# Head norms and rotations of windowed attention laid between the chunks of a Mamba-2 convolution, in a two-layer hybrid backbone on one core

## The reference, cut to what matters

```python
def mixer_cd(h_lat, h_ctx, row, col, ...):
    q_l, k_l, v_l, z_l, xbc_l, dt_l = jnp.split(h_lat @ w_in, cuts, axis=-1)
    q_c, k_c, v_c, z_c, xbc_c, dt_c = jnp.split(h_ctx @ w_in, cuts, axis=-1)
    k_c = rmsnorm(heads(k_c, 2), k_head_g)
    q_lh = rope_2d(rmsnorm(heads(q_l, 8), q_head_g), row, col)
    k_lh = rope_2d(rmsnorm(heads(k_l, 2), k_head_g), row, col)
    attn_l = window_attention(q_lh, k_lh, heads(v_l, 2), k_c, v_c, sink)
    # the other half: u = silu(conv4(xbc)); x (512), B (256), C (256) = split(u)
    # two directions, chunks of 128: y = (C B^T * decay) (x dt) + D x
    y = rmsnorm((ys[0] + ys[1]) * silu(z), norm_g)
    return concat(attn_l, y) @ w_out
```

## Time and profile before

| | |
|---|---|
| median of 3 runs | 1686.78 us (1683.6 to 1687.5) |
| the profiled execution's own time | 1687.27 us |
| its span, first to last instruction | 1685.5 us |
| mean granted TensorE clock | 0.865 of full speed |
| busy: TensorE, VectorE, ScalarE | 74%, 32%, 24% |
| scan's stage, heads' stage, attention (from their first instructions) | 152.6, 22.5, 60.3 us |

### The profile page before, as it was taken

One profiled execution on the slowest core, in us unless ns is written; L12 is line 12 of the kernel. 1 busy time (PEld: TensorE's weight loads), 2 busy tenths in 40 slices (PEclk: granted clock), 3 DMA queues, 4 the chain that ended last, 5 costly groups with the idle time before them and its releaser, 6 DMA issues. The chain is left out here.

```text
span 1685.5 us, 34940 instructions
## 1 busy us (share of the span) xinstructions
PE 1249.5 (74%) x14230; PEld 727.4 (43%) x14231; DVE 541.3 (32%) x1492; ACT 405.3 (24%) x932; POOL 39.3 (2%) x83
## 2 busy tenths in 40 slices
PE   3897888795799997686762999488497675556552
PEld 2454665543465554343431565244255342223221
DVE  0537555515322221121115444863521110111102
ACT  0343224303132321121104123342222221111110
POOL 0001001010000000000002000000000000000000
PEclk8899899997899998899875999758699897777776
DMA  6411988396699999999987210442689999999995
GB/s 254 156 76 45 329 331 305 106 408 254 254 415 428 429 430 428 429 429 429 429 354 256 68 50 0 168 182 88 257 365 428 429 429 429 429 429 429 429 429 217
DMA packets 84160, 515.12 MB, mean 306 GB/s; under 512 B 13917, under 2 KB 18242, under 8 KB 58746
## 3 DMA queue, kind: packets, MB, share of 16 engines
q1 hardware_dynamic: 75248, 489.63, 70.9%
q10 hardware_dynamic: 5146, 13.78, 2.1%
q0 software_dynamic: 3696, 10.73, 1.7%
HBM read 497.10 MB, written 17.01 MB: 305 GB/s over the span
## 5 line engine op out<-in xcount | busy, mean ns | idle before, releaser
L1481 PE MATMUL bank<-sb_ring,sb_scratch 128*32 128x256 f32 x3904 | 271.8, 440 | 150.7 <-DMA sb_ring<-in_moe_w_up 139.3
L1481 PEld LDWEIGHTS bank<-sb_ring,sb_scratch 128*32 128x32 f32 x3904 | 146.4, 126 | 273.6 <-issue 214.2
L1562 DVE TENSOR_TENSOR sb_scratch<-sb_scratch,bank 128x128 f32<-128x128 f32 x88 | 25.4, 288 | 701.2 <-ACT sb_scratch L1515 701.2
L1519 ACT ACTIVATE sb_scratch<-bank 32x256 f32<-32x256 f32 x352 | 131.8, 374 | 273.9 <-PE bank L1491 270.8
L1481 PE MATMUL bank<-sb_scratch 128*32 128x256 f32 x1728 | 117.5, 432 | 63.4 <-DMA sb_scratch<-in_moe_w_up 58.4
L1461 PE MATMUL bank<-sb_h,sb_scratch 128*32 128x256 f32 x2256 | 141.2, 385 | 6.1 <-DVE sb_scratch L1549 6.1
L1515 ACT ACTIVATE sb_scratch<-bank 128x128 f32<-128x128 f32 x88 | 24.4, 277 | 424.5 <-PE bank L1481 424.4
L1491 PE MATMUL bank<-sb_ring,sb_scratch 128*32 128x256 f32 x1856 | 111.5, 380 | 8.6 <-issue 8.2
L1481 PEld LDWEIGHTS bank<-sb_scratch 128*32 128x32 f32 x1728 | 61.5, 124 | 117.9 <-issue 92.7
L1461 PEld LDWEIGHTS bank<-sb_h,sb_scratch 128*32 128x32 f32 x2256 | 75.0, 111 | 54.6 <-DVE sb_scratch L1549 6.6
L1491 PEld LDWEIGHTS bank<-sb_ring,sb_scratch 128*32 128x32 f32 x1856 | 62.7, 110 | 51.2 <-issue 19.0
(11 more groups left out here) (366 smaller groups left out, 1450.4 us busy)
## 6 DMA issues: line engine op xcount, KB each, us to landing
sb_ring<-in_moe_w_gate SPq DMA_DIRECT2D x44, 2048.0 KB, 27.4
sb_ring<-in_moe_w_up SPq DMA_DIRECT2D x44, 2048.0 KB, 32.1
sb_ring<-in_moe_w_down SPq DMA_DIRECT2D x41, 2048.0 KB, 34.5
sb_ring<-in_ada_w SPq DMA_DIRECT2D x20, 2048.0 KB, 14.4
sb_scratch<-in_moe_w_up SPq DMA_DIRECT2D x20, 2048.0 KB, 35.7
sb_scratch<-in_moe_w_gate SPq DMA_DIRECT2D x20, 2048.0 KB, 29.9
sb_scratch<-in_moe_w_down SPq DMA_DIRECT2D x20, 2048.0 KB, 36.2
sorted_out<-sb_scratch ACTq DMA_DIRECT2D x88, 128.0 KB, 6.1
```

The costliest lines, as they stand in the source:

```text
L1481: last = nc.tensor.matmul(c.bank(1, 2, FQ)[MB * q:MB * q + MB, :, :], m.xt[:, k, :], m.gu[j][:, :, k, q * FQ:(q + 1) * FQ], start=k == 0, ...
L1519: last = nc.scalar.activation(m.yb[j][:, q * DQ:(q + 1) * DQ], c.ps[3][MB * q:MB * q + MB, 0:DQ], ACT.Copy)
L1562: v.tensor_tensor(m.hm, m.sg, c.ps[1][:, FQ:2 * FQ], ALU.mult).then_inc(hm_ready, 1)
```

## The change

`swa_heads_stage` is taken out, and its work is put into `project_ssd_stage`; `loads` goes to the attention stage's SyncE. The chunks are in another order: the queries' second, then x, then B and C, then z. TensorE's order becomes: four row units, two query units, x, `cumulate` behind the fourth, B, C, with `turn_inputs` between, then six batches of four head transposes around the four gate units, the products, and a loop without projections. All batches use bank 5, so each waits for ScalarE's copy of the one before. C is projected, copied, convolved and passed through Silu for the 256 latent positions alone. VectorE squares the keys ahead of the convolution, and behind chunks 0, 2, 3, 4 and 5 does one part each of norms and rotations, now for all tiles of a kind together; `work`, their scratch, moves to `ring[0]`. ScalarE takes one Sqrt for all heads behind its second Silu.

```diff
-def conv_channels(c, dst, src, m, w_cols, b_col, width):
+def conv_channels(c, dst, src, m, w_cols, b_col, width, streams=2):
-    out = dst[:, m, :].rearrange("p (s t) -> p s t", s=2)
+    out, src = dst[:, m, :].rearrange("p (s t) -> p s t", s=2)[:, 0:streams], src[:, m, 0:streams]
...
-CHUNKS_CD = [((512, 256), (2304, 16)), ((1280, 512),), ((1792, 512),), ((768, 512),), ((0, 512),)]
+CHUNKS_CD = [((512, 256), (2304, 16)), ((0, 512),), ((1280, 512),), ((1792, 512),), ((768, 512),)]
...
-        self.work = cut(c.ht_flat, 1024, 2, SI)
+        self.work = c.ring[0][:, 6144:6144 + LT * SI]
...
-    ROWS, XBC, GATE, QUERY = 0, 4, 12, 16
+    QUERY, XBC, GATE = 4, 6, 14
+    def wide(j):
+        return 2 if j < 6 else 1
+            sp.wait_ge(product, QUERY)
+            load_cd_chunk(c, sp, w_in, 3)
             sp.wait_ge(product, XBC)
-            load_cd_chunk(c, sp, w_in, 3)
-            sp.wait_ge(product, XBC + 4)
             load_cd_chunk(c, sp, w_in, 4)
...
+            def turn_heads(b):
+                pe.wait_ge(head_ready, (1, 1, 2, 2, 3, 3)[b])
+                if b:
+                    pe.wait_ge(head_copied, b)
+                for slot, (rows, _) in enumerate(batches[b]):
+                    last = nc.tensor.transpose(c.bank(5, 4, P)[0:HD, slot, :], rows, c.ident[:])
+                last.then_inc(head_turned, 1)
...
+            for u in range(XBC):
                 project(u)
+            for j in range(4):
+                copied(pe, j)
+                project(XBC + j)
             pe.wait_ge(a_ready, 1)
             pe.wait_ge(side, SMALL)
+            pe.wait_ge(q_out, 2)
             cumulate()
+            for j in (4, 5):
+                copied(pe, XBC + j - 4)
+                project(XBC + j)
             pe.wait_ge(u_ready, 4)
             turn_inputs(0)
             turn_inputs(1)
+            for j in (6, 7):
+                copied(pe, XBC + j - 4)
+                project(XBC + j)
             turn_inputs(2)
             turn_inputs(3)
+            turn_heads(0)
+            for j in range(4):
+                copied(pe, XBC + 4 + j)
+                project(GATE + j)
+                turn_heads(j + 1)
+            turn_heads(5)
             pe.wait_ge(u_ready, 8)
+            copied(pe, GATE + 1)
             products(1)
...
-            copied(pe, GATE + 3)
-            project(QUERY)
             for w in range(NS // 2):
...
-                if w == 2:
-                    project(QUERY + 1)
                 pair_product(w)
...
+            for t in range(LT):
+                act.wait_ge(product, QUERY + t + 1)
+                nc.scalar.activation(m.q[:, t, :], c.ps[bank_of(QUERY + t)][:], ACT.Copy).then_inc(q_out, 1)
             for j in range(8):
...
+                if j == 1:
+                    act.wait_ge(mean_r, 1)
+                    nc.scalar.activation(ss, ss, ACT.Sqrt).then_inc(root_r, 1)
                 if j in (5, 6):
                     copy_input(2 * (j - 5))
                     copy_input(2 * (j - 5) + 1)
...
+            copy_heads(0)
             for j in range(4):
                 act.wait_ge(product, GATE + j + 1)
                 nc.scalar.activation(m.z[:, j, :], c.ps[bank_of(GATE + j)][:, 0:SEQ], ACT.Silu).then_inc(out_a, 1)
+                copy_heads(j + 1)
+            copy_heads(5)
...
+            between = (square_queries, None, norm_keys, scale_queries, lambda: turn_queries(0), lambda: turn_queries(1), None, None)
+            square_keys()
             for j in range(8):
                 dve.wait_ge(out_a, j + 1)
-                conv_channels(c, m.u, m.xbp, j, ...)
+                conv_channels(c, m.u, m.xbp, j, ..., wide(j))
                 dve.sem_inc(conv_r, 1)
+                if between[j]:
+                    between[j]()
```

More of the change, by code:

```diff
@@ L1802, in project_ssd_stage @@
     S = c.sem
-    ROWS, XBC, GATE, QUERY = 0, 4, 12, 16
-    units = [(0, t) for t in range(NT)] + [(1 + j // 4, j) for j in range(8)] + [(3, j) for j in range(4)] + [(4, t) for t in range(LT)]
+    QUERY, XBC, GATE = 4, 6, 14
+    units = [(0, t) for t in range(NT)] + [(1, t) for t in range(LT)] + [(2 + j // 4, j) for j in range(8)] + [(4, j) for j in range(4)]
     weights_in = [32, 16, 16, 48, 32]
@@ L1814, in project_ssd_stage @@
     NS = 2 * SH
+    mean_r, root_r, head_ready, head_turned, head_copied, q_out = (
+        S(x) for x in ("head_mean", "head_root", "head_ready", "head_turned", "head_t_copied", "queries_copied"))
+    ss_k, ss_q = c.stat[:, 16:16 + NT * KVH], c.stat[:, 16 + NT * KVH:16 + NT * KVH + LT * NH]
+    ss = c.stat[:, 16:16 + NT * KVH + LT * NH]
+    batches = [[(m.kv[:, t, h * HD:(h + 1) * HD], m.kt[0:HD, h, t * P:(t + 1) * P]) for t in (2 * b, 2 * b + 1) for h in range(KVH)] for b in range(2)]
+    batches += [[(m.q[:, t, h * HD:(h + 1) * HD], m.qt[0:HD, h, t * P:(t + 1) * P]) for h in range(4 * b, 4 * b + 4)] for t in range(LT) for b in range(2)]
+    def wide(j):
+        return 2 if j < 6 else 1
     SMALL = 16 * 7
@@ L2012, in _, with copy_heads @@
                     copy_input(2 * (j - 5) + 1)
+            def copy_heads(b):
+                act.wait_ge(head_turned, b + 1)
+                src = c.bank(5, 4, P)[0:HD]
+                if b < 2:
+                    dst = m.kt[0:HD, :, 2 * b * P:(2 * b + 2) * P].rearrange("p h (t n) -> p t h n", t=2)
+                    src = src.rearrange("p (t h) n -> p t h n", t=2)
+                else:
+                    t, h = (b - 2) // 2, (b - 2) % 2 * 4
+                    dst = m.qt[0:HD, h:h + 4, t * P:(t + 1) * P]
+                nc.scalar.activation(dst, src, ACT.Copy).then_inc(head_copied, 1)
+            copy_heads(0)
             for j in range(4):
@@ new lines, in turn_pairs @@
+            def turn_pairs(rows, t, heads):
+                t1, t2 = (m.work[:, j * 256:j * 256 + heads * 32].rearrange("p (h a f) -> p h a f", h=heads, a=2) for j in range(2))
+                rope(c, rows, m.rope[:, 0, t], m.rope[:, 1, t], t1, t2, heads, HD // 4)
+            def norm_keys():
+                dve.wait_ge(root_r, 1)
+                step(v.reciprocal(ss, ss))
+                by_row = ss_k.rearrange("p (t h) -> p t h", t=NT).unsqueeze(3).to_broadcast([P, NT, KVH, HD])
+                step(v.tensor_tensor(k_rows, k_rows, by_row, ALU.mult))
+                for t in range(NT):
+                    step(v.tensor_tensor(k_rows[:, t], k_rows[:, t], m.kg.unsqueeze(1).to_broadcast([P, KVH, HD]), ALU.mult))
+                for t in range(LT):
+                    turn_pairs(k_rows[:, t], t, KVH)
+                dve.sem_inc(head_ready, 1)
@@ L2054, in _ @@
+            square_keys()
             for j in range(8):
                 dve.wait_ge(out_a, j + 1)
-                conv_channels(c, m.u, m.xbp, j, [c.cols_cd[:, 8 * w + j:8 * w + j + 1] for w in range(4)], c.cols_cd[:, 32 + j:33 + j], 4)
+                conv_channels(c, m.u, m.xbp, j, [c.cols_cd[:, 8 * w + j:8 * w + j + 1] for w in range(4)], c.cols_cd[:, 32 + j:33 + j], 4, wide(j))
                 dve.sem_inc(conv_r, 1)
+                if between[j]:
+                    between[j]()
             dve.wait_ge(cum_r, 1)
@@ L2250, in loads @@
             sp.wait_ge(wo_in, 16)
-        swa_heads_stage(c, m, loads)
         units = [(h, t, 0) for t in range(LT) for h in range(NH)]
```

107 lines of the change are left out of this document (22 added, 85 removed).

## The result

The changed kernel takes 1655.14 us (median of 4 runs, 1650.37 to 1657.03) where the kernel before, run beside it, takes 1686.32 (4 runs, 1683.6 to 1687.5): a ratio of 0.9819 [0.9801, 0.9837]. That is 31.2 us faster; forecast were 23.6, with 1657 us as the low end of the range.

What follows compares the result with a forecast made beforehand. The second mixer's time was taken as the sum of its barrier-ended stages, TensorE setting the scan's, with DMA idle: -22.4 + 11.3 - 12.5 = -23.6 us, from 1686.78 to 1663.2 us; range 1657 to 1670 (forecast's own 1660 to 1667).

Steps and rivals of the forecast that it cites:

- The heads' stage goes: Stage between scan and attention, barrier included, is removed: 22.4 us saved.
- TensorE up to the group products: Scan's stage ahead of the products: query units, transposes and waits added, half of C's columns removed; +11.3 us.
- The loop: Scan's loop: both query units leave it, regaining 5.6 and 6.86 us; together -12.5 us.
- SyncE and the transfers: Weight and chunk loads: no wait for chunks; w_out, issued behind the attention's start, is needed at its end.
- The stage's length: Scan's stage was to be 150 to 154 us long if the forecast was right.
- Rivals 2 (waits bite): Scan's stage: waits at head batches add 3.5 us, loop regains only 9 us; 1670 us, chance 0.13.
- 3 (low clock throughout): Loop and attention: TensorE's clock stays low, costing 26 to 27 us; 1690 us, chance 0.03.
- 4 (transfers bound): Whole kernel: transfers were the bound anyway, so no change; 1687 us, chance 0.03.
- I cost this at nothing: Scan's stage: VectorE's head work is covered by TensorE's projecting, 0 us; without that cover 1.5 to 3 us.
- so the attention again starts at 1.2 GHz, and I take the same 60.3 us: Attention: clock has fallen again by its start, so its length is unchanged at 60.3 us; bounds +2.3 and -4.7.
- Rival 1: Attention: the clock rises early because it begins in another phase; further -4.7 us, 1658.5 us, chance 0.11.
- the bound for an early rise: Attention: rising at once spares two or three steps and about 2.5 us of the start, -4.7 us.

Runs made afterwards that it cites:

- the run with C for all: Changed kernel with C projected, copied, convolved and passed through Silu for all 512 positions; 1671.10 us.
- the two fed kernels: Changed kernel and kernel before, each with a spare 512-column TensorE product per attention step and five or three ahead of the attention; 1651.67 and 1675.23 us.
- The warm start: Changed kernel with five spare 512-column products behind the scan's last sum, so TensorE doesn't rest before the attention; 1659.24 us.
- the row with 4.4: Changed kernel with two more vector instructions of 512 columns at the end of the scan's stage; 1659.14 us.

## Why the prediction was right and wrong

**Right, and shown.** *The heads' stage goes*: -22.5 for -22.4. *TensorE up to the group products*: +11.7 between stages in which the clock did the same (90.00 to 101.68) for +11.3; the transposes cost 6 x 0.44 = 2.6 instead of 3.2, the waits 2.0 from start to start instead of 1.2, and the C halves spare the 6.9 forecast (7.4 by the run with C for all, which has a longer wait in it). *The loop*: from the first row to the end -12.4 for -12.5, in both pairs of profiles in which the clock was low equally long there. *SyncE and the transfers*: no wait for a chunk, w_out needed at the attention's end and there. *The stage's length*: 150 to 154 us was named, 150.6 to 153.2 came. And the sum: -22.5 + 11.7 - 12.4 = -23.2 from the parts, and 23.6 us between the two fed kernels, 0.7 of them in the attention, for -23.6. That the second is the forecast to the tenth is luck. Rivals 2 (waits bite), 3 (low clock throughout) and 4 (transfers bound) fell: waits of 2.0 us, a clock of 1.00 from 1038.9 to 1073.1, and a gain.

**Right in kind, short of a term.** "I cost this at nothing", for the head vector work, was 0.7 us by the run without it, and the seventh chunk stands behind a rotation as well as the fourth: the seventh comes 3.5 us behind the sixth, whose convolution and rotation take 2.9 and 2.8. The fall of the clock behind `cumulate` was in no sum. It costs 1.7 us (15.68 for 13.98) and isn't owed to the change: it came in 3 of 6 profiles with before's code in this stage and in 8 of 14 with the new one, but not in the profile that the prediction was read from.

**Wrong.** The step that failed is "so the attention again starts at 1.2 GHz, and I take the same 60.3 us". Its first half held: the clock was 0.50 at the start in all four profiles. The second didn't, since how the attention starts doesn't say how it goes on. It took 50.4 us, -9.8 outright. Rival 1 had the mechanism (the clock rises earlier in the attention, since another phase of it meets the start) and gave it 0.11 and -4.7 us; both too little. Its price failed on the reading of the earlier trace rows: the step of 6.92 us "after it rose" was taken for one at the full clock, and so the bound for an early rise could only be some steps of 0.76 us and a shorter start. The windows of the kernel before shown above, which could have been read then, have the clock at 1.00 and 0.50 by turns in it, and a value product as long as at the low clock (1.98 us) stands in the earlier trace rows itself. A step at the full clock is 5.38 us. With the fed kernel's 47.7 us, which has such steps throughout, as the floor, the bound is 60.2 - 47.7 = 12.5 us, and a range that reaches it goes down to 1651 us.

The Trainium skill (TensorE: Matmul & The Clock Gate, "What's actually happening") says that idleness throttles the engine and sustained activity releases it. The feeding runs agree as far as the second half goes: with one spare product in each step's hole, every step from the first value product on took 5.38 us. The warm start agrees with the first: high clock, TensorE busy 2.56 of 5.00 us, then a fall. But a TensorE busy 15.8 of 16.5 us (after), 24.3 of 25 and 31.6 of 32.3 us (after with one instruction of 128 and with two of 512) stood at 0.50 all the while, so "sustained" doesn't tell when the release comes.

**The cause of the 9.8 us, shown and open.** Shown: it isn't the change's work, since the kernel before does the same attention in 50.4 us when it starts some 1 to 3 us later (178.0 us behind the scan's stage's first issue, not 175.2; 52.8 us when it is 176.3), and in 48.4 when it is fed. It isn't the length of the rest (58 to 59 us four times behind a short one, 50.4 behind the long stage of before), nor chance in the changed kernel's own profiles (four of four alike). Nor is it the transfers that now run beside the attention: the four slow ones behind a short rest had them too. It is the moment at which the attention meets the clock: the added vector instructions change nothing else, and they cost one kernel 3.6 to 8.6 us of attention and gave the other 6.5 to 9.8 (with five of them). The changed kernel happens to end its scan at a good one.

In the table, two things make up the attention's length: how long the clock takes to rise (17, 26 or 34 us), and where in a step it does. Up to 2.16 us behind the value product's start it then holds, for 20.5 us or to the end, and from 2.25 on it alternates. The holes in a step are part of it: where they were filled, no profile of three alternated. But they aren't enough, since the changed kernel has them and held 1.00 for 33 us. That the place of the rise *causes* this is argued from 17 profiles in which nothing contradicts it; no run moved the rise alone. Open too is what decides between 17, 26 and 34 us: by the distance from the last fall alone the row with 4.4 (33.2 us) doesn't go with its neighbour at 3.3 (17.2). And two of the changed kernel's first four executions took 1657 us at a mean clock of 0.870 and 0.871 where the profiled ones had 0.876 and 0.877: perhaps their attentions were longer (the profiles with 58 to 59 us behind a short rest and no added C have 0.869 to 0.871), but they have no trace.

## What to carry to other kernels

Before a duration is taken as "the full clock's", look at the granted clock in windows shorter than a step of the loop, and at the duration of one kind of product on both levels; a mean over a stage hides a clock that rises and falls within a step. A part of the kernel whose time hangs on the clock's moment can gain or lose more than the change under test, so price a change between versions in which that part is held steady, here by one spare product in the hole of each step. Such a feeding is also the robust form: it keeps the attention at 48 us in either kernel, where the plain one took 50 to 60. It is a gain only where the plain one is slow: the kernel before gained 10 us by it, the changed kernel nothing that its runs can tell (1651.67 and 1651.05).

## What the runs showed of the hardware

- The same instructions of one stage took 50.4, 52.8, 54.0, 55.1, 56.7 or up to 60.2 us, by the course of the clock in them. A step of two heads took 5.38 us at 1.00, 7.67 at 0.50, and 6.8 to 7.1 when the clock alternated.
- More work can be a gain: five more vector instructions of 0.72 us each (3.60 us for the five) ahead of the attention shortened the kernel before by 5 to 7 us from the scan's start to the attention's end, in two executions. One instruction of 128 columns (0.3 us) lengthened the changed kernel's attention from 50.4 to 59.0 and 54.0 us.
- A high clock at the start of the attention was worse than a low one (57.3 us against 50.4) where nothing fed the engine, in one execution.
- TensorE, busy for 31.6 of 32.3 us, was left at 0.50 the whole time; and 24 products of 8 columns each (2.74 us) in the middle of a solid stretch were followed by 3.4 us at 0.50 in 11 of 20 profiles.
